# Cache values landed as four heads of eight pages in 2 KB pieces, with the score columns reordered to match, in a one-core hybrid decoder layer

## What is computed

```python
# q: (8 seq, 8 heads, 8 tokens, 64); pool_k, pool_v: (160 pages, 8 heads, 128 tokens, 64)
kmean = seq_block_means(page_table)                    # mean key of each of 8 blocks (256 tokens = 2 pages)
gate  = einsum('bhqd,bhnd->bhqn', q, kmean)
_, idx = lax.top_k(gate, 3)                            # 3 of the 8 blocks are attended, for each head and query
sel_k = pool_k[phys, hsel]; sel_v = pool_v[phys, hsel]
s_sel = einsum('bhqd,bhqkd->bhqk', q, sel_k) * 64**-0.5 - slope * (q_pos - sel_pos)
p     = softmax(concat([s_sel, s_own]))                # own: the new tokens
out   = p_sel @ sel_v + p_own @ own_v
```

## Time and profile before

| | |
|---|---|
| median of 3 runs | 865.55 us (864.74 to 866.35) |
| profiled execution, its own time | 863.19 us |
| span of the profile, first to last instruction | 861.4 us |
| PE busy | 824.6 us (96%) |
| DVE busy | 470.2 us (55%) |
| ACT busy | 339.4 us (39%) |
| moved by DMA | 197.50 MB, mean 229 GB/s |
| share of the chain that ended last: PE, DVE, DMA | 82%, 9%, 3% |

### The profile page before, as it was taken

How to read it: one execution, slowest core, us unless ns; L and a number is a source line. 1 busy time by engine, 2 the same in 40 slices (tenths; PEclk the granted TensorE clock), 3 DMA queues, 4 the chain that set the end, 5 groups by cost and what they waited for, 6 DMA issues and landing times.

```text
span 861.4 us, 17670 instructions
## 1 busy us (share of the span) xinstructions
PE 824.6 (96%) x7084; PEld 739.3 (86%) x7084; DVE 470.2 (55%) x721; ACT 339.4 (39%) x477; POOL 269.9 (31%) x321
## 2 busy tenths in 40 slices
PE   8889999999999999999988989989899999999996
PEld 7789989989899899888665666559799999999996
DVE  3446344344344678535798888349844444443454
ACT  3242333332223585455344342455753333332240
POOL 3251000000002408999999999101100000000030
PEclk9999999999999999999999999999999999999998
DMA  9978867866955435347999999999344444544421
GB/s 296 325 227 280 282 228 279 286 215 215 370 204 201 145 124 196 98 145 242 379 354 319 354 370 357 352 354 377 108 147 147 147 146 146 177 140 165 137 74 62
DMA packets 159797, 197.50 MB, mean 229 GB/s; under 512 B 12099, under 2 KB 133177, under 8 KB 159717
## 3 DMA queue, kind: packets, MB, share of 16 engines
q1 hardware_dynamic: 150637, 187.94, 65.4%
q10 hardware_dynamic: 8800, 8.43, 3.0%
q0 software_dynamic: 288, 0.14, 0.1%
HBM read 193.67 MB, written 3.17 MB: 229 GB/s over the span
## 4 chain that ended last, share of the span: by engine, by line
PE 82%; DVE 9%; DMA 3%; ACT 2%; issue 2%; POOL 1%; SPq 0%; DVEq 0%; ACTq 0%; POOLq 0%
PE bank L1897 18%; PE bank L1899 18%; PE bank L1898 18%; PE bank L2166 5%; PE bank L2191 3%; PE bank L1806 2%; PE bank L2275 2%; DVE kT L1575 2%; DMA araw<-in_w_ada 1%; DMA araw<-in_cache_v 1%; PE bank L1929 1%; PE bank L1785 1%; PE bank L1836 1%; DVE yT L1502 1%; DVE wlo L1240 1%
## 5 line engine op out<-in xcount | busy, mean ns | idle before, releaser
L1240 DVE TENSOR_TENSOR wlo<-raw,whi 128x2048 fp32r<-128x2048 f32 (+1 forms) x74 | 166.0, 2244 | 212.3 <-ACT whi L843 212.2
L1897 PE MATMUL bank<-mh,whi 128*128 128x320 f32 x768 | 239.5, 312 | 0.0
L1899 PE MATMUL bank<-mh,wlo 128*128 128x320 f32 x768 | 237.4, 309 | 0.0
L1898 PE MATMUL bank<-ml,whi 128*128 128x320 f32 x768 | 237.4, 309 | 0.0
L843 ACT CAST whi<-raw 128x2048 fp32r<-128x2048 f32 (+1 forms) x74 | 137.3, 1856 | 194.8 <-PE bank L1899 190.9
L1897 PEld LDWEIGHTS bank<-mh,whi 128*128 128x128 f32 x768 | 144.3, 188 | 5.1 <-issue 5.0
L1898 PEld LDWEIGHTS bank<-ml,whi 128*128 128x128 f32 x768 | 144.3, 188 | 0.1
L1899 PEld LDWEIGHTS bank<-mh,wlo 128*128 128x128 f32 x768 | 144.3, 188 | 0.0
L1897 PE MATMUL bank<-hh,whi 128*128 128x320 f32 x352 | 110.0, 313 | 0.0
L1899 PE MATMUL bank<-hh,wlo 128*128 128x320 f32 x352 | 108.8, 309 | 0.0
L1898 PE MATMUL bank<-hl,whi 128*128 128x320 f32 x352 | 108.8, 309 | 0.0
(11 more groups left out here) (313 smaller groups left out, 1173.5 us busy)
## 6 DMA issues: line engine op xcount, KB each, us to landing
araw<-in_w_ada SPq DMA_DIRECT2D x24, 1024.0 KB, 7.0
raw<-in_ffn_wg SPq DMA_DIRECT2D x19, 1024.0 KB, 8.8
raw<-in_ffn_wu SPq DMA_DIRECT2D x19, 1024.0 KB, 7.7
raw<-in_ffn_wd SPq DMA_DIRECT2D x16, 1024.0 KB, 5.9
raw<-in_cache_k SPq DMA_DIRECT2D x56, 256.0 KB, 4.6
raw<-in_cache_v SPq DMA_DIRECT2D x42, 256.0 KB, 6.8
raw<-in_w_in SPq DMA_DIRECT2D x10, 1024.0 KB, 5.2
aland<-in_w_ada SPq DMA_DIRECT2D x8, 1024.0 KB, 9.8
```

The lines of the kernel that those rows point to most:

```text
L1240: dve.tensor_tensor(wl(slot_w(phase, u))[:, 0:size], landed(phase, u)[:, 0:size], wh(slot_w(phase, u))[:, 0:size].bitcast(F32), ALU.subtra ...
L1897: pe.matmul(bank[:, b, 0:T], wh(slot)[:, c], h_, start=(start and n == 0), stop=False)
L1898: pe.matmul(bank[:, b, 0:T], wh(slot)[:, c], l_, start=False, stop=False)
L1899: ins = pe.matmul(bank[:, b, 0:T], wl(slot)[:, c], h_, start=False, stop=(stop and n == len(parts) - 1))
```

## The change

A value chunk still has 1 MB, but it now holds four heads (`h = 4 * (kvi % 2)`) of eight pages, where it held eight heads of four pages. A partition takes 8 consecutive tokens (`r=8`), so a piece is 2 KB, as for the keys. A page's four heads fill 16 partitions, every fourth one of a half of the slot: pages with even `y` in partitions 0 to 63, odd ones in 64 to 127. A value DMA so has 16 x 4 pieces of 2 KB, 128 KB, and a chunk has eight DMAs: six from SP, two from the ACT queue. The slots' semaphores count 128 for a value chunk and 64 for a key chunk (`kv_landed` replaces `kv_turn`). The score columns are reordered to match: the copies to `kT` write runs of 128 columns instead of every second one, the score matmuls read runs of 16 columns instead of 32, a constant table follows. PE has the same number of matmuls of the same size on a value chunk, in another order.

```diff
-    c[:, C_POS:C_POS + 4 * P] = (wide // P % 2 * P + wide % P // 4 * 4 + 2 * (wide // 256))[None, :]
+    c[:, C_POS:C_POS + 4 * P] = (wide % P // 64 * P + wide % 64 // 4 * 8 + 4 * (wide // P % 2) + 2 * (wide // 256))[None, :]
...
-def kv_turn(kvi):
-
-    return sum(kv_slot(n) == kv_slot(kvi) for n in range(kvi))
+def kv_landed(kvi):
+
+    return sum(64 if kv_chunk(n)[0] == "k" else 128 for n in range(kvi + 1) if kv_slot(n) == kv_slot(kvi))
...
-            return kT[:, k % 2, 1024 * half:1024 * half + 1024].rearrange("p (x n q) -> p x q n", x=4, q=2)
+            return kT[:, k % 2, 1024 * half:1024 * half + 1024].rearrange("p (q x n) -> p x q n", x=4, q=2)
...
+        def load_values(eng, kvi, page, ys):
+
+
+            slot = kv_raw(kvi)
+            h = 4 * (kvi % 2)
+            for y in ys:
+                at = 64 * (y % 2)
+                src = i["cache_v"][0][bass.ds(page[y], 1)][:, h:h + 4]
+                eng.dma_start(slot[at + y // 2:at + 64:4, :].rearrange("p (h f) -> p h f", h=4),
+                              src.rearrange("a h (g r) d -> g (a h) (r d)", r=8)).then_inc(kv_in[kv_slot(kvi)], 16)
...
-                load_pages(sp, cache, kvi, numbers[8 * (k % 4 // 2) + k % 2:], range(3 if cache == "v" else 4))
+                if cache == "k":
+                    load_keys(sp, kvi, numbers[8 * (k % 4 // 2) + k % 2:])
+                else:
+                    load_values(sp, kvi, numbers[8 * (k % 4 // 2):], range(6))
...
-                load_pages(act, "v", kvi, page[8 * (k % 4 // 2) + k % 2:], range(3, 4))
+                load_values(act, kvi, page[8 * (k % 4 // 2):], range(6, 8))
...
-                pe.wait_ge(kv_in[kv_slot(kvi)], 64 * (kv_turn(kvi) + 1))
+                pe.wait_ge(kv_in[kv_slot(kvi)], kv_landed(kvi))
...
-                        at = 512 * (r % 2) + 256 * (x % 2) + 128 * (x // 2)
+                        at = 512 * (r % 2) + P * x
...
-                    values = kv_raw(kvi).rearrange("p (h f) -> p h f", h=NH)
-                    for i_ in range(2):
-                        at = P * (8 * b2 + 2 * c + i_)
-                        for g4 in range(NHP):
+                    values = kv_raw(kvi).rearrange("p (h f) -> p h f", h=4)
+                    for i_ in range(4):
+                        at = P * (8 * b2 + 4 * (c // 2) + i_)
+                        t = P * (2 * (i_ % 2) + i_ // 2)
+                        for n in range(2):
+                            g4 = 2 * (c % 2) + n
```

More of the change, by code:

```diff
@@ L479, in page_numbers, with load_keys @@
             return page
-        def load_pages(eng, cache, kvi, page, xs=range(4)):
+        def load_keys(eng, kvi, page):
             slot = kv_raw(kvi)
[L484 to L490, removed]
+            for x in range(4):
+                src = i["cache_k"][0][bass.ds(page[2 * x], 1)]
+                eng.dma_start(slot[:, 512 * x:512 * x + 512], src.rearrange("a h (g r) d -> (a h g) (r d)", r=8)).then_inc(kv_in[kv_slot(kvi)], 16)
+        def load_values(eng, kvi, page, ys):
[6 more added lines that the diff above has]
+                              src.rearrange("a h (g r) d -> g (a h) (r d)", r=8)).then_inc(kv_in[kv_slot(kvi)], 16)
         @block.sync
@@ L2185, in scores @@
                         pe.wait_ge(pt_evac, 5 * j)
-                keys = kT[:, k % 2, :].rearrange("p (i x h n) -> p i x h n", i=2, x=4, h=NH)
+                keys = kT[:, k % 2, :].rearrange("p (i x h n) -> p i x h n", i=4, x=4, h=NH)
                 for e in range(2):
@@ L2189, in scores @@
                         h = 2 * g4 + e
-                        out = bank[QG * g4:QG * g4 + QG, 4 + g % 2, :].rearrange("p (i c n x) -> p i c x n", i=2, c=2, x=4)[:, :, k % 2]
+                        out = bank[QG * g4:QG * g4 + QG, 4 + g % 2, :].rearrange("p (i c n x) -> p i c x n", i=4, c=2, x=4)[:, :, k % 2]
                         ins = pe.matmul(out, qb[:, 2 * j + k // 4, h, :], keys[:, :, :, h, :], start=e == 0, stop=e == 1)
@@ L2270, in pair_values @@
                         pe.wait_ge(pt_evac, 5 * j + k // 2 + 1)
-                    values = kv_raw(kvi).rearrange("p (h f) -> p h f", h=NH)
-                    for i_ in range(2):
-                        at = P * (8 * b2 + 2 * c + i_)
-                        for g4 in range(NHP):
+                    values = kv_raw(kvi).rearrange("p (h f) -> p h f", h=4)
[4 more added lines that the diff above has]
+                            g4 = 2 * (c % 2) + n
                             ins = pe.matmul(bank[QG * g4:QG * g4 + QG, 7, 256 * b2:256 * b2 + 256].rearrange("p (e f) -> p e f", e=2),
-                                            pT[:, at + QG * g4:at + QG * g4 + QG], values[:, 2 * g4:2 * g4 + 2, P * i_:P * i_ + P],
-                                            start=(c == 0 and i_ == 0), stop=False)
+                                            pT[:, at + QG * g4:at + QG * g4 + QG], values[:, 2 * n:2 * n + 2, t:t + P],
+                                            start=(c < 2 and i_ == 0), stop=False)
                     ins.then_inc(v_used, 1)
```

## The result

The changed kernel takes 916.94 us (median of four runs) against 865.14 us for the kernel before on the same chip: a ratio of 1.0597, 95% interval 1.0576 to 1.0617, so slower by 52 us. The forecast was 912.5 us with a range of 863 to 924. The profiled execution took 915.07 us (before 863.19), 51.9 us more.

The account below looks back on a forecast made before the run. SP's queue was to bound the value groups: its 199.1 us of issues end 52.9 us later, less 5.6 us given back behind the last issue, net 47.3 us; on 865.55 us this gives 912.5 us, range 863 to 924 us.

Parts of the forecast that it names:

- The mechanism: Value groups: SP must issue 192 value DMAs instead of 96, so its last value issue comes 52.9 us later.
- The possible gain: Value transfers: 2 KB pieces at 389 instead of 350 GB/s, up to 9.6 us if transfers alone counted.
- rival 1: SP's value loads: issue about 0.30 us, transfers bound again, some 4 us gained, 861.5 us; chance 16 in 100.
- Issue of the new form: SP's queue: each new value load takes 0.602 us to issue, 0.787 us from one to the next, 151.1 us for 192.
- The argument by layout: SP's value loads: same tile, source and step of four partitions as the present load, so the same issue time, 0.602 us.
- the rival by count of partitions: SP's value loads: 16 partitions cost between 8 (0.30 us) and 30 (0.47 us); kept for rivals, chances 16 and 11 in 100.
- The rest of SP's sum: SP's queue besides values: key DMAs 33.1 us, page numbers 10.8, conv stores about 3.4, w_out load about 0.7.
- The tail: Last value chunk: PE starts 3 us after SP's last issue ends, instead of 8.6 us, giving back 5.6 us.
- PE's order booked at nothing: PE's value matmuls: the new order over heads has the same number of instructions and the same waits, so costs nothing.
- Rival 4: Value transfers: a DMA reaching half the partitions halves the write rate, 22 to 41 us more, 935 to 953 us; 4 in 100.
- rivals 1 to 3: SP's value-load issue: about 0.30 us, 861.5 us (16 in 100); 0.33 to 0.36, no change (5); near 0.469, 887 us (11).
- PE's waits and its clock: Value groups: PE waits some 3.7 us for most value chunks; up to 11 us more for lower clock or held key copies.

Follow-up runs that it names:

- the doubling alone: The kernel before with each value page loaded by two DMAs of four heads instead of one, pieces still 1 KB: 923.13 us, ratio 1.0667.
- the two ways to relieve SP: The changed kernel with a chunk's value DMAs split four on SP, four on ACT: ratio 1.0427; the changed kernel with constant page numbers: 1.0391.
- the two runs above: The kernel before with value pages landing as keys do, 128 partitions x 2 KB: 861.17 us; and with 2 KB pieces on its 32 partitions: 861.02 us.
- the probe: The kernel before, with SP issuing eleven forms of small value load twice each behind its last store; issue times read, no kernel time given.
- columns-only kernel: The changed kernel with the value loads of before put back, keeping the new score columns and PE's order over heads: 875.37 us, ratio 1.0145.
- the pairing: The changed kernel with PE taking two value chunks together, going round all four column groups: 918.4 us, ratio 1.0646.

## Why the prediction held, step by step

**The mechanism.** SP's queue sets the pace of the value groups: shown by the doubling alone (1.0667), by the two ways to relieve SP (both back to 1.04), by the chain, and by the share of 0.55 where SP's loads are alone.

**The possible gain.** This reading was wrong: that the transfers bound the whole stage before, so that 10% in rate are 9.6 us. With 2 KB pieces and no dearer issue the two runs above gained 2 to 4 us. The chain of before from 380 to 620 us (the view cuts this line off at its end) says why:

```profile
by line: PE bank L2166 19.0%; PE bank L2191 10.2%; PE bank L2275 6.5%; DVE kT L1575 6.1%; issue 5.7%; DMA araw<-in_cache_v 4.3%; DVE yT L1502 3.5%; DVE yT L1500 3.2%; PE bank L2013 3.1%; POOL tmp L733 1.9%; DVE gsum L1558 1.6%; DVE wlo L124
```

DMAs of the cache have 4.3% of it, against 19.0% for PE's key transposes and 10.2% for its score matmuls. The sum does not use the 9.6 us, and rival 1 took only 4 us of them, which the two runs bear out.

**Issue of the new form.** Booked at 0.602 us and a step of 0.787; measured 0.557 and 0.741. The argument by layout was right and the rival by count of partitions wrong, as the probe showed: with a step of four, 16 partitions cost about as much as 32. The number of engines that a DMA goes to, which the prediction also weighed, does not set it: the same 16 partitions cost 0.33 to 0.43 or 0.59 to 0.62 us by their step. The term 192 x 0.787 = 151.1 us was 151.8 us in the trace: 142.3 us in steps, 7.5 us in longer issues, nearly all in 14 of them, and 2.0 us in longer gaps between issues. What held these up is not shown. The sum is what I booked, by luck: a step that was too dear made up for delays that I had not booked.

**The rest of SP's sum.** Keys 37.5 us instead of 33.1, since 17 of 64 issues were held up, 4.2 us; page numbers 11.6 instead of 10.8; conv stores and `w_out` 4.4 instead of 4.1. Together 205.3 us instead of 199.1. With a start 1 us earlier, the end is 625.2 instead of 620.0 us.

**The tail.** 3 us booked, 2.0 measured (625.16 to 627.19). Together 51.4 us for the last chunk where 47.3 were forecast, then 0.85 us more inside it, of which 0.5 us reaches the end.

**PE's order booked at nothing.** This step was wrong: it costs 0.85 us for each of most value chunks. The columns-only kernel lost 12.7 us, of which going round all four groups gave back 7.9 us by the ratios; the rest has no shown cause. "The same number of instructions" was no argument, since their overlap depends on which column groups they alternate between. In the change this cost lies within the wait for SP's loads, and the pairing gained nothing.

**The share of the DMA engines.** I expected about 0.6 at 220 GB/s. Over the groups the rate was 243 to 253 and the share 0.86 to 0.97, since ACT's loads and late keys land there too and a packet took 0.117 us and not 0.088; where SP's loads were alone it was 0.55 at 170 GB/s. Rival 4 had part of the truth: the transfers of this form are slower, though not halved. How far a cheaper issue alone would have carried rivals 1 to 3 is therefore open; the best time of the change's form seen here is 898.6 us. The landing of 4.7 us, not 3 to 4, goes with the slower packets.

**PE's waits and its clock.** Not 3.7 us for each of most chunks: PE waited for value loads 26 times, 44.4 us in all, and for the first eight chunks not at all. After such waits its granted clock fell, to 0.52 from 604 to 613 us, where two chunks took 3.63 us each instead of 1.92. The allowance of up to 11 us for this was not used, since the last chunk waited for its load anyway and ran in 1.92 us.

**Copies.** DVE's is unchanged (1,224 ns). ACT's contiguous write is 0.1 us faster, where I had allowed for 0.1 us of loss:

```profile
L1126 ACT COPY kT<-bank x32: 992/1013/1020, 395.0 to 561.0; 128x1024 f32<-128x1024 f32 x32
```

**The rule on issuing engines** that the prediction weighed, of the Trainium skill ("DMA: Bandwidth & Descriptors", Issuing engines are not separate DMA queues), speaks of an issue that is usually small beside its DMA. At 0.741 us of queue for 128 KB this kernel is outside it. The prediction called that a reading of the trace before, which it was not: there 0.787 us went with a DMA of 256 KB, which takes 0.75 us at 350 GB/s.

No version tried beats the kernel before by more than 0.5%, and the two that gain at all have the values in places where PE can't use them.

## What to carry to other kernels

Before making the pieces of a transfer bigger, count DMAs per megabyte and multiply by the queue's own step: here 192 DMAs at 0.74 us in place of 96 at 0.79 put 67 us more on SP's queue and made the kernel 52 us slower, to win at most 4. Take the price of an issue from a row with the same step between partitions, and look at rate and share together afterwards: a low rate at a high share says that the packets themselves are slow, and that a cheaper issue will help only so far. Issues moved to another engine's queue stand in front of that engine's own work. When operands are cut differently, check that PE still goes round all its column groups.

## What the hardware showed that was not expected

- For 16 partitions the time of an issue goes with the step between them: adjacent ones 0.317 us, every fourth 0.557 (0.595 with a constant address). It is not the step alone: 8 partitions with a step of four took 0.72 to 0.79, and 32 or 64 adjacent ones 0.42 to 0.60.
- DMAs to 16 partitions moved 2 KB pieces in 0.106 us and more, those to 32 or 128 partitions in 0.088; sixteen adjacent partitions are the worst, 0.186 us and 190 GB/s.
- Sixteen matmuls of 379 ns take 1.07 us when they go round four column groups and 1.92 us when they go round two.
- 64 matmuls in a row, four chunks, took 3.66 us before and 4.62 us with two groups a chunk, since neighbouring chunks use different groups and overlap: the loss is largest where chunks come singly.
